# Two-block transformer on one core: the opening norm's scale and shift as columns, its sums shared by two engines

## The reference, cut to what matters

```python
cond = jax.nn.silu(c)
mod = (cond @ ada_w[l] + ada_b[l])[:, None, :]
sh1, sc1, g1, sh2, sc2, g2 = jnp.split(mod, 6, axis=-1)
h = rmsnorm(x, norm1_g[l]) * (1 + sc1) + sh1
x = x + g1 * hybrid_mixer(h, cos, sin, w_in[l], ...)   # begins with h @ w_in[l] + b_in[l]
```

## Time and profile before

| | before |
|---|---|
| median of three runs | 1480.53 us |
| the profiled execution | 1479.98 us |
| its span on the core | 1478.2 us |
| TensorE busy | 1450.4 us, 98% |
| GpSimd busy | 1203.2 us, 81% |
| ScalarE busy | 744.9 us, 50% |
| VectorE busy | 720.7 us, 49% |

### The profile page before, as it was taken

The page is one execution under the profiler, slowest core; times in us unless marked ns, Lnnn a source line. Parts: engine busy times, 40 slices in busy tenths (PEclk is TensorE's granted clock), DMA queues, the critical chain, the costliest instruction groups (busy, mean ns, idle before and its releaser), DMA issues.

```text
span 1478.2 us, 21666 instructions
## 1 busy us (share of the span) xinstructions
PE 1450.4 (98%) x7666; PEld 1214.7 (82%) x7666; DVE 720.7 (49%) x1575; ACT 744.9 (50%) x1242; POOL 1203.2 (81%) x978
## 2 busy tenths in 40 slices
PE   7999999999999999999999999999999999999997
PEld 4898777799988988777888888778888887788886
DVE  7663664766643754745566214364650044655202
ACT  3335674644444435765544445465654345555441
POOL 4799988888878977558998989908999978489994
PEclk9999999999999999999999999999999999999999
DMA  9995547688875986337775566704555757156561
GB/s 357 387 349 177 174 161 233 223 312 312 309 264 176 394 296 215 114 98 238 236 241 186 192 199 172 239 29 157 188 193 196 221 155 226 62 163 202 192 199 57
DMA packets 149685, 313.87 MB, mean 212 GB/s; under 512 B 10933, under 2 KB 31817, under 8 KB 149577
## 3 DMA queue, kind: packets, MB, share of 16 engines
q1 hardware_dynamic: 147824, 311.15, 62.9%
q10 hardware_dynamic: 1754, 1.35, 0.3%
HBM read 311.39 MB, written 1.06 MB: 211 GB/s over the span
## 4 chain that ended last, share of the span: by engine, by line
PE 93%; DVE 3%; ACT 2%; POOL 1%; issue 1%; DMA 0%; SPq 0%; DVEq 0%; ACTq 0%
PE bank L776 58%; PE bank L821 12%; PE bank L822 8%; PE bank L819 5%; PE bank L1006 1%; PE bank L986 1%; PE bank L1022 1%; POOL lo_units L730 1%; PE bank L857 1%; PE bank L966 1%; DVE bank L1668 1%; ACT hi_units L1294 1%; PE bank L953 1%; PE bank L1009 1%; PE bank L1107 0%
## 5 line engine op out<-in xcount | busy, mean ns | idle before, releaser
L730 POOL TENSOR_TENSOR lo_units<-raw_units,hi_units 128x512 fp32r<-128x512 f32 (+3 forms) x928 | 1150.6, 1276 | 233.1 <-ACT hi_units L1294 232.2
L1294 ACT ACTIVATE hi_units<-raw_units 128x1024 fp32r<-128x1024 f32 (+1 forms) x470 | 483.3, 1031 | 434.4 <-PE bank L776 271.1
L776 PE MATMUL bank<-hi_units,turned 128*128 128x512 f32 (+3 forms) x1600 | 438.3, 388 | 1.5 <-DVE turned L1716 0.8
L776 PEld LDWEIGHTS bank<-hi_units,turned 128*128 128x128 f32 x1600 | 292.7, 188 | 52.7 <-issue 3.1
L822 PE MATMUL bank<-turned,lo_units 128*128 128x256 f32 x1024 | 288.2, 281 | 0.0
L776 PE MATMUL bank<-hi_units,turned_wide 128*128 128x512 f32 x992 | 274.5, 391 | 0.0
L821 PE MATMUL bank<-turned,hi_units 128*128 128x512 f32 x736 | 260.6, 399 | 0.0
L776 PE MATMUL bank<-lo_units,turned 128*128 128x512 f32 (+3 forms) x800 | 252.6, 383 | 0.8 <-POOL lo_units L730 0.5
L776 PEld LDWEIGHTS bank<-hi_units,turned_wide 128*128 128x128 f32 x992 | 185.3, 188 | 38.5 <-issue 0.5
L822 PEld LDWEIGHTS bank<-turned,lo_units 128*128 128x128 f32 x1024 | 194.3, 190 | 0.2
L776 PEld LDWEIGHTS bank<-lo_units,turned 128*128 128x128 f32 x800 | 149.8, 188 | 29.9 <-POOL lo_units L730 3.2
(11 more groups left out here) (264 smaller groups left out, 1325.6 us busy)
## 6 DMA issues: line engine op xcount, KB each, us to landing
ada_units<-in_ada_w SPq DMA_DIRECT2D x88, 512.0 KB, 7.8
raw_units<-in_w_ffn_tiles SPq DMA_DIRECT2D x72, 512.0 KB, 5.3
raw_units<-in_mlp_w_out SPq DMA_DIRECT2D x64, 512.0 KB, 3.3
raw_units<-in_mlp_w_tiles SPq DMA_DIRECT2D x56, 512.0 KB, 3.3
raw_units<-in_w_in SPq DMA_DIRECT2D x56, 458.0 KB, 9.8
raw_units<-in_w_in SPq DMA_DIRECT2D x48, 512.0 KB, 6.6
raw_units<-in_w_ffn_out SPq DMA_DIRECT2D x44, 512.0 KB, 3.8
raw_units<-in_moba_w_qkv SPq DMA_DIRECT2D x24, 512.0 KB, 3.8
```

The lines of the kernel that those rows point to most:

```text
L730: pool.tensor_tensor(LO[:, s, b, 0:w], RAW[:, u["slot"], b, 0:w], HI_[:, s, b, 0:w].bitcast(F32), ALU.subtract).then_inc(lo_ready.sem, lo_ ...
L776: ins = pe.matmul(BANK[2 * c["pair"] + t][:, 0:w], (A[a] if A is BT else A[:, a])[:, part, t * P:(t + 1) * P], W[:, s, b, 0:w], start=(i = ...
L1294: act.activation(HI_[:, s, 0:n, 0:w], RAW[:, u["slot"], 0:n, 0:w], ACT.Copy)\
```

## The change

The scale and the shift of the first norm are both made as columns (one value for each partition of the turned rows), in one bank, and the gain is turned into columns too. ScalarE makes unit rows (`x` times the inverse root), TensorE turns them, and VectorE then applies scale and shift in place, in PSUM (`first_columns`). ScalarE and VectorE take the high and low parts from that. GpSimd no longer multiplies rows by `norm1_g`, and its broadcast transfers are gone; the vector comes once as a row of 4 KB. Three of the sixteen units of `ada_w` (units 1 and 3 of `scale0`, unit 1 of `shift0`) go to TensorE as products with one moving column (`column_products`); the other thirteen are VectorE's, among them all of `scale1`. The bias of `ada_b` enters in VectorE's first operation of each chunk. The root of the squares no longer goes by VectorE; the sine and cosine on ScalarE come after `first_hi(0)`. Of the ten products that `keep_running` issued (1 + 1 + 1 + 5 + 2), one is left.

```diff
+PE_UNITS = {(0, 2, 1), (0, 2, 3), (0, 0, 1)}
-    stream.extend(scale0["units"] + [norm1_g(0, 0)] + shift0["units"])
+    stream.extend(scale0["units"] + shift0["units"])
-            stream.extend(c0["units"][0:2] + scale1["units"] + [norm1_g(0, 1)] + c1["units"][0:1] + shift1["units"][0:2])
-            stream.extend(c1["units"][1:2] + shift1["units"][2:4])
+            stream.extend(c0["units"][0:2] + scale1["units"][0:2] + c1["units"][0:1] + scale1["units"][2:4] + shift1["units"][0:1])
+            stream.extend(c1["units"][1:2] + shift1["units"][1:4])
...
-        def gain_rows(half):
...
+        def gain_columns():
+            pe.wait_ge(first_gain_in, 16)
+            for j in range(KT):
+                pe.matmul(columns[:, 2 * KT + j:2 * KT + j + 1], GAIN_ROW[:, j * P:(j + 1) * P], ONES[0:1, 0:1], start=j == 0, stop=False)
+        def column_products(c, i):
+            u = c["units"][i]
+            at = KT if c["key"][2] >= 2 else 0
+            pe.wait_ge(ada_in[u["home"]][u["slot"]], 16 * (u["turn"] + 1))
+            for k in range(UNIT_K):
+                for j in range(4):
+                    ins = pe.matmul(columns[:, at + j:at + j + 1], ada_raw(u)[:, k, j * P:(j + 1) * P], COND[:, i * UNIT_K + k:i * UNIT_K + k + 1],
+                                    start=False, stop=False)
+            ins.then_inc(ada_multiplied.sem, ada_multiplied.mark(u["index"]))
+        def column_sums(c):
...
+            for j in range(4):
+                ins = pe.matmul(columns[:, at + j:at + j + 1], MOD[:, n * CW + j * P:n * CW + (j + 1) * P], ONES[:, 0:1],
...
+        pe.wait_ge(rows.sem, rows.at("cond"))
+        gain_columns()
+        column_products(scale0, 1)
         keep_running(1)
...
+        column_products(scale0, 3)
+        column_sums(scale0)
...
                 turn(tag, O, range(4), 0, ready)
                 turn(tag, O, range(4), 1, ready)
-                keep_running(5)
-                pe.wait_ge(ada_used.sem, ada_used.at(shift0["units"][-1]["index"]))
-                shift_sum(0, BANK[1])
-                keep_running(2)
+                column_products(shift0, 1)
+                column_sums(shift0)
                 for i in (0, 1):
                     pe.wait_ge(turned_lo.sem, turned_lo.at((tag, i)))
                     unit(c0, i, HT)
-                second_scale(scale1, BANK[SB_[0]])
-                unit(c1, 0, HT)
                 turn(tag, O, range(4), 2, ready)
                 turn(tag, O, range(4), 3, ready)
-                pe.wait_ge(ada_used.sem, ada_used.at(shift1["units"][-1]["index"]))
-                shift_sum(1, BANK[SB_[1]])
-                unit(c1, 1, HT)
+                unit(c1, 0, HT)
+                pe.wait_ge(rows.sem, rows.at(("columns", 0)))
+                column_sums(scale1)
+                unit(c1, 1, HT, only=0)
+                column_sums(shift1)
+                unit(c1, 1, HT, only=1)
...
+        def unit_rows(half):
+            act.wait_ge(rows.sem, rows.at("inverse root"))
+            cols = slice(half * CW, (half + 1) * CW)
+            for t in range(NT):
+                ins = act.activation(O[:, t, cols], X[:, t, cols], ACT.Copy, scale=RR[:, t:t + 1])
...
+        act.dma_start(GAIN_ROW, dram["norm1_g"][0:1, :]).then_inc(first_gain_in, 16)
...
+                    if kt == 0 and (u["l"], u["c"]) in FIRST_BANK:
+                        dve.wait_ge(cleared.sem, cleared.at("second shift"))
                         dve.wait_ge(first_bias_in, 16)
...
+        def first_columns(half):
+            columns, cols = BANK[SB_[1]], slice(4 * half, 4 * half + 4)
+            dve.wait_ge(product.sem, product.at(("columns", half)))
+            if half == 0:
+                link(v.tensor_copy(GAIN, columns[:, 2 * KT:3 * KT]))
+            v.tensor_copy(SHIFT[:, cols], columns[:, cols])
+            say(v.scalar_tensor_tensor(GAINED[:, cols], columns[:, KT + 4 * half:KT + 4 * half + 4], 1.0, GAIN[:, cols], ALU.add, ALU.mult),
+                ("columns", half))
             for g in (2 * half, 2 * half + 1):
-                dve.wait_ge(turned_hi.sem, turned_hi.at((("n1", 0), g)))
+                dve.wait_ge(turned.sem, turned.at((("n1", 0), g)))
                 for k in (2 * g, 2 * g + 1):
+                    part = BANK[(TQ, TP)[g % 2]][:, k % 2 * S:(k % 2 + 1) * S]
+                    ins = v.tensor_scalar(part, part, GAINED[:, k:k + 1], SHIFT[:, k:k + 1], ALU.mult, ALU.add)
+                say(ins, ("whole", g))
+            turn_lo(("n1", 0), HT, part=slice(2 * half, 2 * half + 2))
...
-        sums_upto(2)
+        sums_upto(1)
         tables()
         angles()
-        sums_upto(4)
-        root_of_squares(("n1", 0))
-        first_rows(0)
-        sums_upto(8)
+        sums_upto(2)
+        dve.wait_ge(act_side.sem, act_side.at(("root", ("n1", 0))))
+        say(v.reciprocal(RR[:, 0:NT], RSTD), "inverse root")
+        sums_upto(5)
         for l in range(DEPTH):
             if l == 0:
-                first_shift(0)
-                first_lo(0)
-                sums_upto(12)
-                first_rows(1)
-                first_shift(1)
-                first_lo(1)
+                first_columns(0)
+                sums_upto(13)
+                first_columns(1)
```

## The result

| | before | after |
|---|---|---|
| median, same chip (10 runs each) | 1480.08 us | 1483.78 us |
| ratio to before, 95% interval | | 1.0022, 1.0014 to 1.0030 |
| the profiled execution | 1479.98 us | 1484.26 us |
| S, start of c0 unit 0 | 29.19 | 31.20 |
| U, start of c0 unit 2 | 49.17 | 50.54 |

The change makes the kernel 3.7 us slower, where 6.9 us faster was forecast and 1482.3 was the far end of the range. The ratio and its interval put the loss at 2.1 to 4.4 us. Three marks are enough to follow it. I add the third one, called W here (c0 unit 3), because the two k-tiles behind U turned out to differ as well: W moved by 3.57 us, and the time by 3.7. The marks are those of one profiled execution.

The account below looks back on a forecast made before the run. TensorE's unbroken projection from U was taken to set the end, with VectorE's sums deciding S and U. S = 25.1 plus 17.2 put U at 42.3 instead of 49.17: 6.9 us off, 1473.6 us, range 1472.6 to 1482.3.

Parts of the forecast that it names:

- A: The forecast itself: TensorE's upper clock level is there in time, 6.9 us off, 4.5 with slow first units; chance 0.48.
- B: Rival: TensorE's clock stays low until c0, columns at 28.9, S = 32.0, U = 49.2, 0.0 us gained; chance 0.27.
- the upper level: TensorE's 2.4 GHz clock, at which eight records of one-column products take 1.05 us.
- the lower level: TensorE's 1.2 GHz clock, at which eight records of one-column products take 1.86 us.
- the 6.9 us: Forecast gain: U, start of c0 unit 2, moves from 49.17 to 42.3, and the end moves with it.
- The tail from the columns to S: First half: copies, scale, scalings, high and low parts between reading the columns at 22.2 and S = 25.1.
- S + 17.2: Forecast place of U: VectorE's eight units (12.5 us), reading and tail in the second half, giving 42.3.
- the reading: VectorE reading the finished columns from TensorE, put 1.2 us after VectorE's sums, as in the old kernel.
- the tail: Second half: the same steps as in the first, from the columns' reading at 39.5 to U; 2.8 us.
- the second half: Stretch from S to U, bound by VectorE's units, with TensorE waiting 2.6 us in all.
- D: Rival: later weights come no earlier than by the missing broadcasts, TensorE falls back to them, 1.2 to 2 us remain; chance 0.05.
- C: Rival: the clock rises on the way, with the idle product or the turns, about 3.5 us off; chance 0.10.
- E: Rival: low clock and gain row late at 9.0, S 34.5, U 54.1, 4.9 us slower; chance 0.10.

Follow-up runs that it names:

- e2_warm: Changed kernel with three idle 512-column products ahead of the gain products, in place of the one behind them; +2.7 us against the kernel before (1482.25).
- v2: `v1` with unit 1 of `scale1` given to TensorE in the second half and two idle products behind it instead of four; -4.2 us against before (1475.59).
- e7_one_operand: Changed kernel with the bias left out of `shift1`, so its first VectorE operation reads one large operand; +2.3 us against before (1482.11).
- e1_hold: Changed kernel with two idle 480-column products ahead of the wait for VectorE's last sum in the second half; +2.2 us against before (1481.75).
- v1: Changed kernel with all sums on VectorE, rope angles later, TensorE's waits filled with idle products; -4.4 us against before (1475.09).
- b1_no_idle: Kernel before with all ten `keep_running` products taken out and nothing else; +3.2 us against before (1482.81).
- e3_all_vector: Changed kernel with all sixteen units of sums on VectorE, the one idle product kept; +0.4 us against before (1479.99).
- e6_shared_fast: Changed kernel, sharing kept, idle products between blocks of one-column products, c1 unit 1 whole behind the last sum; +2.3 us against before (1481.83).
- v1_again: The same kernel as `v1`, in a second series beside `v2`; -4.8 us against before (1474.95).

## Why the prediction was wrong

**The step that failed is the choice between A and B.** The forecast took the upper level to be there in time (0.48) against B (0.27). It priced 36 column products at 9.5 us and had them lie beside VectorE's work, with only the last four waiting. In fact TensorE needed 20.6 us from the gain row on, at the lower level, and ended at 27.8, 7.5 us behind VectorE's sums (20.34): the overlap that the 6.9 us rested on wasn't there. The marks that it had set for itself decide it: eight records of one-column products took 1.85, not 1.05; the copy of `first_columns(0)` waited 7.58 us on TensorE ("about 8" for B, 1.2 for A); S is 31.20 (32.0 for B, 25.1 for A). What spoke for A was that TensorE works without a break and on weights of 128 rows. `e2_warm` and `v2` show that this isn't enough: behind 512-column products the level was up, and unbroken one-column products let it fall. The Trainium skill's sentence in "TensorE: Matmul & The Clock Gate", section "Part 1: The HAM clock gate (the "warmup" mystery)", that activity releases the throttle, doesn't help here; 20.6 us of unbroken work, nearly all of it one-column products, stayed at the lower level. The row of the kernel before that spoke against it, unbroken work to 14.86 with a slow product at its end, was the better guide.

**B itself was too kind.** It gave W at 51.7 (49.2 + 2.5) and 0 to 1 us of loss. Measured is 55.24, 3.5 later, in these terms:
- S came 0.8 earlier than B had it. The gain row landed at 7.21 instead of 6.5. From there to the end of the last sum it was 20.6 us instead of 22.4: I had added busy times of groups (1.86 for 8 records), but neighbouring groups overlap, and from start to start eight records are 1.70. The tail from the columns to S is 3.4 instead of 3.1.
- U came at S + 19.34 instead of S + 17.2. VectorE was free at S + 0.7, as said. Its eight units took 13.5 instead of 12.5 (the operation of 1.65 us, `e7_one_operand`); the reading came 2.0 behind them instead of 1.2 (the last sum at the lower level); the tail was 3.1 instead of 2.8.
- The two k-tiles behind U took 4.7 instead of 2.5. No rival had the level fall a second time. The forecast had said that TensorE waits 2.6 us in the second half, and treated that wait as room for slow units. It is the opposite, for it is in or behind such waits that the level falls: 1.9 us here, 1.83 in `e1_hold`. The length of the wait alone doesn't decide it: in `e7_one_operand` the level fell behind 0.64 us and eight one-column records, in `v1` it didn't behind 1.29 us that followed three idle 512-column products (the wait ended at 21.89). Why it falls in one case and not in the other stays open. I had cited the Trainium skill, "TensorE: Matmul & The Clock Gate", section "Loop structure matters more than you think", on waits between matmuls, for the first half only; the trace agrees with it in the second.

**What was right.** The bias row landed at 8.08 (8.4), in part by luck: it was issued at 2.85, not 3.7, and took 5.2 us instead of 4.8; in the other runs of this kind it came between 7.1 and 8.1. VectorE's own sums for the first half ended at 20.34 (21.0); the second half is set by VectorE's units; nothing was given back behind 55 us, so D falls. C falls with A, for no product ahead of S was at the upper level. E had its gain row at 9.0 and S at 34.5; neither came, and its sign was right for another reason.

**The change in three parts.** The runs split the 3.7 us, each difference being uncertain by 1.3 to 2 us. Taking out the idle products costs 3.2 (`b1_no_idle` against before). Scale and shift as columns, all sums on VectorE, give back 2.8 (`e3_all_vector` against `b1_no_idle`). Sharing the sums with TensorE costs the remaining 3.3 (after against `e3_all_vector`). It relieved VectorE of three units, 4.7 us, but put 48 records of one-column products, 10 us at the lower level, on the other engine, which became the late one.

Open is how the level would behave with one-column products spread thinner than in `e6_shared_fast`. Also, the profiled execution after is 4.3 us longer than the one before while W moved by 3.6. The 0.7 is less than the spread of the runs (1482.7 to 1485.2), and I found no place for it.

## What to carry to other kernels

Before a product moves to TensorE, ask at which level it will run, and whether it will keep the level for what follows. A chain of one-column products was dear by itself (0.43 us a product at the lower level) and cost the big products behind it their clock. Idle time of TensorE ahead of dense work isn't free room: fill it, or it may be paid again in the first k-tiles behind it. When two engines share a sum, first work out which one is late at the lower level.

## What the runs showed of the hardware

- A wait of 1.9 us behind 458-column work was enough for the granted clock to fall (44.9 after). It came back only 10 us later (55.2), although dense work had begun at 47.2, with one wait of 0.69 in it.
- The granted clock of the windows reads 1.00 for the opening in every kernel, also where durations are those of the lower level. It reads 0.50 only behind a first fall (`e2_warm` from 16, after from 45). The level of the opening has to be read from durations.
- The same kernel (`v1`, `v1_again`) kept the upper level through the first half in one profiled execution and lost it for 3.4 us in another.
- A VectorE operation with two large operands in SBUF took 0.8 to 0.9 us longer while a GpSimd subtraction was running (1.56 to 1.70 against 0.76), while those with one operand in PSUM ran through (six in 4.71 us, at 32.71 after). Small operations on 128x16 elements took 1.1 us each in `v1` while GpSimd was subtracting (47.14 to 51.6), and 0.18 right behind it; nobody waited for them.
- Between idle products, sixteen one-column records took 1.84 us at the upper level, against 3.41 at the lower.
